# First block's attentions: the two heads' score products, one head behind the other instead of alternately

## The reference, cut to what matters

```python
s_loc = jnp.einsum('bnqhgd,bnkhd->bnhgqk', qb, kw) * SCALE_A      # window
s_ctx = jnp.einsum('bnqhgd,blhd->bnhgql', qb, k_ctx) * SCALE_A
...
s = (jnp.einsum('bqhd,bkhd->bhqk', q_n, keys_n)                   # latent
     + jnp.einsum('bqhd,bkd->bhqk', q_r, keys_r))
p = jax.nn.softmax(s * SCALE_B, axis=-1)
return jnp.einsum('bhqk,bkhd->bqhd', p, vals)
```

## Time and profile before

| | |
|---|---|
| Median of the runs shown | 3434.1 us (3421.6 to 3436.0, three runs) |
| The profiled execution | 3425.2 us, span 3423.4 us |
| TensorE busy | 3157.3 us (92%) |
| VectorE, ScalarE, GpSimd busy | 44%, 34%, 30% |
| Mean granted TensorE clock | 0.96 |
| HBM read | 274.7 MB, 81 GB/s over the span |

### The profile page before, as it was taken

How to read it: one execution, slowest core, us unless ns; L and a number is a source line. 1 busy time by engine, 2 the same in 40 slices (tenths; PEclk the granted TensorE clock), 3 DMA queues, 4 the chain that set the end, 5 groups by cost and what they waited for, 6 DMA issues and landing times.

```text
span 3423.4 us, 44451 instructions
## 1 busy us (share of the span) xinstructions
PE 3157.3 (92%) x18095; PEld 2461.8 (72%) x18095; DVE 1512.1 (44%) x1800; ACT 1169.3 (34%) x1874; POOL 1042.4 (30%) x489
## 2 busy tenths in 40 slices
PE   5989899999999699888899889989999899989999
PEld 2767468888888477466677567767887677668887
DVE  3343335454221544334431377547663475644420
ACT  3235332112123335332223344544332344634432
POOL 0301003332333131023345332124554322135553
PEclk8999899999999799999999999999999999999999
DMA  4201003343222111025543221215665322023333
GB/s 175 56 13 40 1 13 99 105 117 93 62 62 61 32 38 39 1 73 161 160 116 91 79 62 44 58 44 172 187 179 155 90 56 82 2 68 99 99 93 93
DMA packets 440053, 279.71 MB, mean 82 GB/s; under 512 B 113466, under 2 KB 419244, under 8 KB 439468
## 3 DMA queue, kind: packets, MB, share of 16 engines
q1 hardware_dynamic: 439852, 276.87, 28.6%
HBM read 274.73 MB, written 2.10 MB: 81 GB/s over the span
## 4 chain that ended last, share of the span: by engine, by line
PE 61%; DVE 5%; ACT 3%; POOL 3%; issue 3%; DMA 1%; SPq 0%; ACTq 0%; DVEq 0%; POOLq 0%
PE ps L609 44%; PE ps L1048 3%; POOL WL L1890 3%; PE ps L1124 1%; PE ps L1146 1%; PE ps L1117 1%; ACT WH L1408 1%; PE ps L867 1%; PE ps L1183 1%; DVE GV L2062 1%; PE ps L871 1%; ACT PR L1484 1%; DVE RSTD L2046 1%; DVE HL L2055 1%; PE ps L652 1%
## 5 line engine op out<-in xcount | busy, mean ns | idle before, releaser
L1890 POOL TENSOR_TENSOR WL<-RAW,WH 128x1024 fp32r<-128x1024 f32 (+2 forms) x366 | 873.9, 2388 | 2049.8 <-ACT WH L1408 2044.9
L609 PE MATMUL ps<-HH,WH 128*128 128x512 f32 x2296 | 785.4, 379 | 93.5 <-DVE HL L2055 47.1
L609 PE MATMUL ps<-HL,WH 128*128 128x512 f32 x2296 | 771.6, 373 | 0.0
L609 PE MATMUL ps<-HH,WL 128*128 128x512 f32 x2296 | 769.8, 372 | 0.0
L609 PEld LDWEIGHTS ps<-HH,WH 128*128 128x128 f32 x2296 | 403.0, 191 | 205.3 <-POOL WL L1890 58.0
L1408 ACT ACTIVATE WH<-RAW 128x1024 fp32r<-128x1024 f32 (+2 forms) x366 | 377.3, 1031 | 464.7 <-PE ps L609 257.4
L609 PEld LDWEIGHTS ps<-HH,WL 128*128 128x128 f32 x2296 | 403.7, 192 | 77.4
L609 PEld LDWEIGHTS ps<-HL,WH 128*128 128x128 f32 x2296 | 403.4, 192 | 71.5 <-issue 0.7
L2114 DVE SCALAR_TENSOR_TENSOR MSUM<-RAW,CS,MSUM 128x1024 f32<-128x1024 f32 x91 | 157.4, 1755 | 24.8 <-DMA RAW<-in_w_ada 21.8
L609 PE MATMUL ps<-FH,WH 128*128 128x512 f32 x352 | 138.0, 392 | 2.8 <-POOL WL L1890 2.7
L609 PE MATMUL ps<-FL,WH 128*128 128x512 f32 x352 | 137.1, 389 | 0.0
(11 more groups left out here) (351 smaller groups left out, 5010.6 us busy)
## 6 DMA issues: line engine op xcount, KB each, us to landing
RAW<-in_w_in SPq DMA_DIRECT2D x122, 512.0 KB, 3.8
RAW<-in_w_ada SPq DMA_DIRECT2D x96, 512.0 KB, 4.0
RAW<-in_w_up SPq DMA_DIRECT2D x88, 512.0 KB, 4.6
RAW<-in_w_in SPq DMA_DIRECT2D x72, 256.0 KB, 3.7
RAW<-in_w_mod SPq DMA_DIRECT2D x32, 512.0 KB, 3.7
RAW<-in_w_down SPq DMA_DIRECT2D x32, 512.0 KB, 3.9
WMOD<-in_w_mod SPq DMA_DIRECT2D x4, 2048.0 KB, 19.0
RAW<-in_w_branch SPq DMA_DIRECT2D x16, 512.0 KB, 3.4
```

What stands on the lines that cost most here:

```text
L609: ins = nc.tensor.matmul(ps[0:width, t0:t0 + tn], a, b[:, k0 + k, t0:t0 + tn], start=first and k == 0 and i == 0, stop=last and k == kt - ...
L1890: nc.gpsimd.tensor_tensor(WL[s % NWS][:, 0:used], RAW[n % NRAW][:, 0:used], WH[s % NWS][:, 0:used].bitcast(F32), ALU.subtract).then_inc(*u ...
```

## The change

In both `scores` functions of the TensorE program the loop over the heads goes outside and that over the key stretches inside. The same products are issued with the same operands, and the semaphore is still raised by the last product of each head. The waits ahead of them are the same. Before, each stretch was issued for both heads before the next; now all of head 0 comes first, then all of head 1. In a unit with one stretch the order of the window attention stays as it was; in the latent attention the 32-row product of head 0 now precedes the 64-row product of head 1 there too.

```diff
-                    qs, c = slice(qb * P, (qb + 1) * P), 0
-                    for i, (start, m) in enumerate(keys):
-                        for h in range(2):
-                            hs = slice(64 * h, 64 * h + 64)
+                    qs = slice(qb * P, (qb + 1) * P)
+                    for h in range(2):
+                        hs, g, c = slice(64 * h, 64 * h + 64), 32 * ((2 * j + h) % 4), 0
+                        for start, m in keys:
                             nc.tensor.matmul(halves[h][:, c:c + m], QNP[hs, j, qs], KNP[hs, j, start:start + m],
                                              start=True, stop=False)
-                        for h in range(2):
-                            g = 32 * ((2 * j + h) % 4)
                             ins = nc.tensor.matmul(halves[h][:, c:c + m], QRP[g:g + 32, j // 2, qs],
                                                    KR[g:g + 32, start:start + m], start=False, stop=True,
                                                    tile_position=(g, 0))
-                            if i == len(keys) - 1:
-                                ins.then_inc(*up(product_ready, ("B", l, n, "s", h)))
-                        c += m
+                            c += m
+                        ins.then_inc(*up(product_ready, ("B", l, n, "s", h)))
...
-                    c = 0
-                    for i, (start, m) in enumerate(keys):
-                        for h in range(2):
-                            hs = slice(64 * h, 64 * h + 64)
+                    for h in range(2):
+                        hs, c = slice(64 * h, 64 * h + 64), 0
+                        for start, m in keys:
                             ins = nc.tensor.matmul(halves[h][:, c:c + m], QA[hs, j, qb * P:(qb + 1) * P],
                                                    KA[hs, start:start + m], start=True, stop=True)
-                            if i == len(keys) - 1:
-                                ins.then_inc(*up(product_ready, ("A", l, n, "s", h)))
-                        c += m
+                            c += m
+                        ins.then_inc(*up(product_ready, ("A", l, n, "s", h)))
```

## The result

The changed kernel takes 3656.7 us in the median of four runs (3652.7 to 3661.0), the kernel before 3429.1 (3421.6 to 3436.0): a ratio of 1.067, 95% interval 1.065 to 1.0695. The forecast was 3685 us, with a range of 3555 to 3745. The profiled execution took 3655.2 us, 230.0 more than that of before; the sum of the forecast had +256.

A forecast was written before the change was run, and what follows sets the result against it. TensorE, busy 92% of the span, was taken to bound the kernel. The profiled 3425.2 us + 221 latent + 35 window gave 3681, placed at 3685 us between the profiled and median bases; range 3555 to 3745.

The forecast's parts named there:

- Heads serial in the latent part, +118.3 at the high clock: Latent attention scores: head 1 cannot run beside head 0, so score time doubles, 118.3 us more over 32 and 8 units.
- An earlier maximum gains nothing: Latent units: head 0's maximum under head 1's scores brings nothing, except in each layer's first unit.
- the ring: 768-key latent unit, repeating every 7.01 us: scores, first transposes, ScalarE's copy, two exponentials, only then the next scores.
- The small gain of the first units (-1.8): First latent unit of each layer, without transposes: its 3.11 us wait shortens by one maximum, 0.91; in all -1.8 us.
- Half of the units at the low clock, +122: Latent attention: 16 of 32 units run at the low clock, each costing 7.65 us more; bounds four and all 32.
- the 380.4 that the sum had for the high clock: Both latent stages after the change, all at the high clock: 263.9 + 118.3 - 1.8 = 380.4 us.
- Latent part +221: Both latent stages together: 281.8 us before, 502.8 after; bounds +128 and +343.
- Window part +35: Window attention stages: 27 us for partly lost head overlap plus 8 for low clock; bounds 0 and +45.
- the 8 that I added: Window stages: 8 us for four low-clock units losing 1.15 more each and a later clock rise.
- the clock stays: Rival: clock remains as now; latent part +128, window part about +30, total 3583 us; chance 0.17.
- The queue looks far enough ahead: Rival: TensorE takes head 1's products from behind head 0's, so nothing changes, 3423 us; chance 0.07.
- The low clock takes nearly every unit: Rival: nearly all latent units run low, latent part up to +343, total 3813 us (3747 with three quarters); chance 0.08.

The follow-up runs named there:

- the second kernel: Changed kernel's serial latent heads, but each score product takes all 128 rows instead of its head's 64 or 32, window attention unspecified; whole 26 us above the kernel before.

## Why the prediction was right, point by point

- *Heads serial in the latent part, +118.3 at the high clock*: right, and for the reason given. Head 0's scores take 3.35 us at the high clock, and only then head 1's start. Grouped by rows, with head 0 still first in each group, the heads overlap again.
- *An earlier maximum gains nothing*: right, as the ring starts behind head 1's scores. The small gain of the first units (-1.8) is there too: their wait for the exponentials was 3.11 us in both layers and is 2.17 (ahead of 358.58 and of 1504.38), 1.9 in all.
- *Half of the units at the low clock, +122*: right in size. The stages measure 499.7 us; less the 380.4 that the sum had for the high clock, and divided by 7.65, this is 15.6 low units where 16 were taken. In place of half of the units wholly low, every 768-key unit runs low for a part: the highest mean is 0.79 (415.55 to 425.87), others are 0.65 (442.73 to 457.22) and 0.52 (425.87 to 442.73), and only the 256-key units stay high (1.00 from 405.28 to 415.55). The number was an estimate; that it came out this near is partly luck. The reason given, rows without work, is borne out: leaving half of the rows idle lowers the clock with score stretches of the same length (0.88 to 0.75 in layer 0), and filling them raises it (0.69 to 0.99), though the second kernel also has no change of rows.
- *Latent part +221*: measured +217.9.
- *Window part +35*: this is the term that was mis-sized; it measured +17.4. The step that failed took the look-ahead to be one record, because the trace of before showed no more. It is three. A unit of 256 + 256 keys was charged 0.44 us or more and pays nothing. The scores of 128 + 256 + 128 take 0.32 us more and those of 256 + 256 + 128 0.53, where 0.9 to 1.1, or that less one last product, were forecast. And not all of it reaches the stage: in layer 0 a unit of 128 + 256 + 128 keys still takes 2.75 us (242.95 to 245.70), because its longer scores only use up a wait for VectorE; in layer 1 it takes 3.82 for 3.49. That makes 16 x 0.53 + 4 x 0.33 = 9.8 us at the high clock. The other 7.6 go with the lower clock at the start of both stages (0.90 and 0.89 for 0.94 and 0.95 before), near the 8 that I added; some 3 of them are no effect of the change, as the two stages together take 150.0 us in the execution of before and 153.1 and 153.2 in two others whose window scores take no longer than before.
- *The rivals*: "the clock stays" (3583) falls with the granted clock of 0.69 and 0.68. "The queue looks far enough ahead" is true of the window units with two stretches. Its threshold was put rightly for a three-stretch window unit, where five records are needed and the queue has three; the rival overlooked that two stretches need only three. In the latent part a change of rows stops it already in the 256-key units; a 768-key unit would in any case need seven. "The low clock takes nearly every unit" came true of the units, but not of their length: together they run low as long as 15.6 whole ones would. The Trainium skill's statement (TensorE: Matmul & The Clock Gate, Part 3) that products keep their order doesn't hold here: head 1's first starts 0.06 us or less behind head 0's first (253.74), ahead of three that were issued earlier. The 64-deep window that the same part gives for pulling weight loads ahead isn't the limit that showed here; that was three records.
- *The sum*: 3425.2 + 221 + 35 = 3681 against a profiled 3655.2. Of the 26 us, 18 are the window part, 3 the latent part, 5 the rest of the kernel.

## What to carry to other kernels

In these runs, products on different rows of TensorE overlapped only where no more than three records of the first's rows waited ahead of the second, and where no product with another row count stood between them. So put equal row counts together first, and alternate the tiles inside a group where a run would get longer than four records. In the profile, hold count x mean duration of a group against its busy time: 163 against 70.7 us is overlap, and its loss shows there at once. Price rows that lie idle twice, once in time and once in the clock of everything that runs in the same stretch: of the 218 us here, the serial scores are 116 at the high clock (32 x 3.32 + 8 x 1.23), and the clock makes up the other 102.

## What the runs showed of the hardware

- The granted clock didn't follow TensorE's busy share. With half of the score products left out, the latent stage of layer 0 was busy for 93% and had 0.75, where it had been 90% and 0.88 (0.88 to 0.90 in four executions); with serial heads on all rows it was busy for 90% and had 0.99. Removing work made this stage 15 us longer (158.3 to 173.7). The expectation for that kernel had 175 us.
- The Trainium skill (TensorE: Matmul & The Clock Gate, Part 1) describes the gate as following how busy TensorE is; in these runs that alone doesn't put the stages in order.
- The look-ahead past products for the same rows is three waiting records, counted in records and not in columns (1.08 us for four records a head, 1.64 for eight with the same columns).
- A change between 64 and 32 rows costs 0.2 us at the high clock, and nothing behind it started early in any of these kernels, even where the two products share no row.
